# Two mixing blocks on one core: part of the first experts' weights loaded before the last attention values, router products and an embedding product reordered, the first expert's products put between the halves of its gather

## The reference, cut to what matters

```python
for i in range(DEPTH):                       # 2 layers
    h = rmsnorm_2(x, norm_mix[i]); proj = h @ w_in[i]
    y_a = neighbourhood_attention(...) @ w_na_o[i]
    y_b = latent_attention(...) @ w_mla_o[i]
    x = x + (sigmoid(gate_a) * y_a + sigmoid(gate_b) * y_b) @ w_out[i]
    x = x + expert_choice_moe(rmsnorm_2(x, norm_moe[i]), w_router[i], w1[i], w3[i], w2[i])
    x = x + sigmoid(rmsnorm_2(x, norm_ple[i]) @ ple_gate_w[i]) * (p[i] @ ple_w[i])

def expert_choice_moe(h, w_router, w1, w3, w2):      # 16 experts, 32 tokens each
    aff = softmax(h @ w_router)
    vals, idx = top_k(aff.T, 32); xg = h[idx]
    out = (silu(xg @ w1) * (xg @ w3)) @ w2           # each matrix 1024 x 1024, 4 MB
    return zeros.at[idx].add(out * vals)
```

## Time and profile before

| | us |
|---|---|
| median of 3 runs | 1897.53 |
| lowest and highest | 1896.41, 1899.77 |
| time of the profiled execution | 1900.6 |
| span of the profiled execution | 1898.8 |
| TensorE matmul busy | 1550.6 (82%) |
| VectorE busy | 612.3 (32%) |
| ScalarE busy | 500.4 (26%) |
| GpSimd busy | 193.9 (10%) |
| mean HBM traffic | 298 GB/s over the span |

### The profile page before, as it was taken

One profiled execution on the slowest core, in us unless ns is written; L12 is line 12 of the kernel. 1 busy time (PEld: TensorE's weight loads), 2 busy tenths in 40 slices (PEclk: granted clock), 3 DMA queues, 4 the chain that ended last, 5 costly groups with the idle time before them and its releaser, 6 DMA issues.

```text
span 1898.8 us, 29516 instructions
## 1 busy us (share of the span) xinstructions
PE 1550.6 (82%) x12506; PEld 1135.1 (60%) x12506; DVE 612.3 (32%) x923; ACT 500.4 (26%) x910; POOL 193.9 (10%) x214
## 2 busy tenths in 40 slices
PE   7999999999999999665655656999998666666656
PEld 6999899998898886232322323997883322323225
DVE  3456534577556353000000002655450000000005
ACT  3433333556444432000000002454330000000003
POOL 0043000011041100000000002410100000000003
PEclk9999999999999999898888888999999888989888
DMA  8564549432554569999999999545399999999994
GB/s 284 164 219 168 195 155 301 152 111 91 178 172 136 177 233 386 425 427 424 427 426 424 427 426 377 180 152 178 128 378 394 426 425 424 427 425 427 426 425 152
DMA packets 166894, 563.65 MB, mean 297 GB/s; under 512 B 10559, under 2 KB 120027, under 8 KB 133896
## 3 DMA queue, kind: packets, MB, share of 16 engines
q1 hardware_dynamic: 159012, 552.08, 75.1%
q10 hardware_dynamic: 7780, 10.10, 1.6%
HBM read 561.08 MB, written 5.23 MB: 298 GB/s over the span
## 4 chain that ended last, share of the span: by engine, by line
PE 52%; DMA 36%; DVE 4%; ACT 3%; issue 3%; POOL 1%; SPq 0%; ACTq 0%; DVEq 0%; POOLq 0%
DMA ring<-in_moe_w 36%; PE bank L965 21%; PE bank L1213 7%; PE bank L1622 5%; PE bank L921 4%; PE bank L1060 3%; PE bank L1645 2%; PE bank L1276 2%; ACT ring_r L1695 1%; ACT big L1743 1%; PE bank L1090 1%; PE bank L1480 1%; PE bank L1285 1%; PE bank L1037 1%; PE bank L1651 1%
## 5 line engine op out<-in xcount | busy, mean ns | idle before, releaser
L1622 PE MATMUL bank<-ring,big 128*32 128x256 f32 x3840 | 281.3, 443 | 195.7 <-DMA ring<-in_moe_w 193.2
L1622 PEld LDWEIGHTS bank<-ring,big 128*32 128x32 f32 x3840 | 147.0, 123 | 335.8 <-issue 295.4
L965 PE MATMUL bank<-big_r,ring_r 128*128 128x256 f32 (+1 forms) x2760 | 344.1, 285 | 0.0
L965 PEld LDWEIGHTS bank<-big_r,ring_r 128*128 128x128 f32 (+1 forms) x2760 | 335.1, 191 | 3.0 <-issue 2.2
L2092 DVE TENSOR_TENSOR ring_r<-ring,ring_r 128x2048 fp32r<-128x2048 f32 (+2 forms) x105 | 243.0, 2319 | 135.3 <-ACT ring_r L1695 133.9
L1743 ACT ACTIVATE big<-bank 128x512 f32<-128x512 f32 (+2 forms) x186 | 87.9, 491 | 571.6 <-PE bank L921 366.8
L1695 ACT ACTIVATE ring_r<-ring 128x2048 fp32r<-128x2048 f32 (+2 forms) x109 | 204.2, 1881 | 10.4 <-DMA ring<-in_ev_w_out 5.1
L1645 PE MATMUL bank<-ring,big 128*32 128x512 f32 x1024 | 136.7, 634 | 74.0 <-DMA ring<-in_moe_w 55.5
L2479 DVE SCALAR_TENSOR_TENSOR big<-big,bank 128x256 f32<-128x256 f32 x32 | 13.5, 421 | 463.9 <-ACT big L1995 463.9
L1213 PE MATMUL bank<-ring_r,big_r 128*128 128x512 f32 x576 | 135.7, 395 | 0.7 <-DVE big_r L2099 0.7
L921 PE MATMUL bank<-big 128*128 128x128 f32 (+6 forms) x636 | 105.1, 292 | 35.7 <-ACT big L1743 18.2
(11 more groups left out here) (204 smaller groups left out, 1512.8 us busy)
## 6 DMA issues: line engine op xcount, KB each, us to landing
ring<-in_moe_w SPq DMA_DIRECT2D x120, 2048.0 KB, 23.7
ring<-in_moe_w SPq DMA_DIRECT2D x128, 1024.0 KB, 24.9
ring<-in_w_in SPq DMA_DIRECT2D x28, 1024.0 KB, 5.4
ring<-in_od_w_in SPq DMA_DIRECT2D x22, 1024.0 KB, 6.5
ring<-in_ev_w_in SPq DMA_DIRECT2D x20, 1024.0 KB, 7.3
big<-in_moe_w SPq DMA_DIRECT2D x8, 2048.0 KB, 11.2
ring<-in_ev_w_out SPq DMA_DIRECT2D x8, 1024.0 KB, 5.0
ring<-in_od_cmp_w SPq DMA_DIRECT2D x8, 1024.0 KB, 8.1
```

The lines of the kernel that those rows point to most:

```text
L965: ins = unit[0].mark(mm(dst, lhsT, rhs, start=start and n == 0, stop=stop and n == len(terms) - 1))
L1622: ins = mm(banks[5 + up][32 * j:32 * j + 32, 0:256], xg[:, k, q, :], wv[:, r, 256 * j:256 * (j + 1)], start=k == 0, stop=k == KC - 1)
```

## The change

It has five parts, in each of the two layers.

1. SyncE: ahead of the load of `ple_w` (unit `("pw", 0)`) it waits for the last scores (`sc_done`) and then loads three quarters of spare 1 (`spare(1, r0=1)`, 1.5 MB) and all of spare 2 (2 MB). Where both were loaded, after the last values, only the remaining quarter of spare 1 is (`spare_row(1)`, 0.5 MB).
2. TensorE: the logits of tile 0 are made in pieces of 2 and 6 chunks instead of 4 and 4; the logits of tile 1 come ahead of `embed(0)`, which comes after `aff_T(0)`, and `embed(1)` comes after `aff_T(1)`.
3. TensorE: the gather is cut after 6 of its 8 chunks. In the first batch the order is gather 0 to 5, first half of `w1`, gather 6 and 7, first half of `w3`, second half of `w1`, second half of `w3`. In the later batches the order is gather 0 to 5, first half of `w1`, gather 6 and 7, and the rest as it was.
4. The second half of the gather goes to bank 7 instead of bank 6.
5. VectorE: the first batch is written out ahead of the loop, which runs over three batches.

```diff
+                    if unit == ("pw", 0):
+                        sp.wait_ge(sc_done, att_at(l, NAH + MLH))
+                        spare(1, r0=1)
+                        spare(2)
...
                 sp.wait_ge(pv_read, att_at(l, NAH + MLH))
-                spare(1)
-                spare(2)
+                spare_row(1)
                 deep(ups[0], first, 4)
                 sp.wait_ge(merged, 4 * (l + 1))
                 spare(0)
...
                 raw_T(l, 1, 0)
-                logits(l, 0, 0, 4)
+                logits(l, 0, 0, 2)
                 raw_T(l, 1, 1)
-                logits(l, 0, 4)
+                logits(l, 0, 2)
...
+                logits(l, 1)
                 unit[0] = Unit()
                 wait_bank(l, "pw", 0)
-                embed(0)
-                logits(l, 1)
...
                 aff_T(0)
+                embed(0)
+                aff_T(1).then_inc(rtT, 1)
                 embed(1).then_inc(proj_done, 1)
-                aff_T(1).then_inc(rtT, 1)
                 project(l, "pw", 1)
...
+                    def gather(k0, k1):
+                        for k in range(k0, k1):
+                            for t in range(TT):
+                                ins = mm(banks[4 + 3 * (k // 4)][:, (k % 4) * P:(k % 4 + 1) * P], u[:, t, k * P:(k + 1) * P],
+                                         onehot[:, t].rearrange("p q s -> p (q s)"), start=t == 0, stop=t == TT - 1)
+                            if k % 4 == 3:
+                                ins.then_inc(gathered, 1)
+
+                    gather(0, 6)
                     for q in range(BATCH):
                         m = l * NE + b * BATCH + q
...
+                        order = list(itertools.product(range(2), range(2)))
+                        if q == 0 and isinstance(b, int):
+                            order.sort(key=lambda e: e[1])
+                        for up, part in order:
+                            if q == 0 and part == up == 0:
+                                pe.wait_ge(xg_ready, 2 * g4 + 1)
+                            elif q == 0 and (up, part) == order[1]:
+                                gather(6, 8)
+                            if q == 0 and part == 1 and up == 0:
+                                pe.wait_ge(xg_ready, 2 * g4 + 2)
...
-                with dve.Fori(0, NE // BATCH) as b:
+                def batch(b):
...
+                batch(0)
+                with dve.Fori(0, NE // BATCH - 1) as b:
+                    steps.enter(b, BATCH)
+                    batch(b + 1)
+                    steps.leave(NE // BATCH - 1)
```

More of the change, by code:

```diff
@@ L787, in _, with spare, spare_row @@
             for l in range(LAYERS):
+                first = l * NE * D
+                ups = [a["moe_w1_2"], a["moe_w3_2"]]
+                def spare(i, r0=0):
+                    row = first + (i // 2) * D + 512
+                    src = flat(ups[i % 2])[row:row + 4 * P, :].rearrange("(p r) c -> p (r c)", r=4)
+                    sp.dma_start(view(spare_at[i], P, 4 * D)[:, D * r0:], src[:, D * r0:]).then_inc(spare_in[i], 16)
+                def spare_row(i):
+                    row = first + (i // 2) * D + 512
+                    src = flat(ups[i % 2])[row:row + 4 * P, :].rearrange("(p r) c -> p (r c)", r=4)
+                    sp.dma_start(view(spare_at[i], P, D), src[:, 0:D]).then_inc(spare_in[i], 16)
                 for unit in LAYER_UNITS:
+                    if unit == ("pw", 0):
+                        sp.wait_ge(sc_done, att_at(l, NAH + MLH))
+                        spare(1, r0=1)
+                        spare(2)
                     name, i = unit[0], unit[1]
@@ L803, in _ @@
                         tall_l(a["w_out_2"], l, D, 0, D, OUT_ROWS[2][unit[2]][0], 256, split=True)
[L804 to L810, removed]
                 def down(row):
@@ L909, in __init__ @@
                 def __init__(s, l, i):
-                    pe.wait_ge(spare_in[i], 16 * (l + 1))
+                    pe.wait_ge(spare_in[i], 16 * (2 if i == 1 else 1) * (l + 1))
                     s.words, s.first, s.step = view(spare_at[i], P, 4, D), True, Unit.before
@@ L1610, in batch @@
+                    gather(0, 6)
                     for q in range(BATCH):
                         m = l * NE + b * BATCH + q
[L1612 to L1625, removed]
+                        order = list(itertools.product(range(2), range(2)))
[8 more added lines that the diff above has]
+                                pe.wait_ge(xg_ready, 2 * g4 + 2)
+                            spare = isinstance(b, int) and q < 2 and part == 1
+                            U = Spare(l, 2 * q + up) if spare else Unit(double=True)
+                            wv = U.at(P, 4, D)
+                            for r in range(4):
+                                k = 4 * part + r
+                                for j in range(4):
+                                    ins = mm(banks[5 + up][32 * j:32 * j + 32, 0:256], xg[:, k, q, :],
+                                             wv[:, r, 256 * j:256 * (j + 1)], start=k == 0, stop=k == KC - 1)
+                                    U.mark(ins)
+                            if part == 1:
+                                ins.then_inc(up_done, 1)
@@ L2462, in _ @@
                 stand(dve)
-                with dve.Fori(0, NE // BATCH) as b:
+                def batch(b):
                     g4 = l * (NE // BATCH) + b
-                    steps.enter(b, BATCH)
                     V.tensor_tensor(onehot, con("iota").unsqueeze(1).unsqueeze(1).broadcast_to([P, TT, BATCH, CAP]),
-                                    idxT[:, :, bass.ds(b * BATCH, BATCH)].unsqueeze(3)
+                                    (idxT[:, :, b * BATCH:(b + 1) * BATCH] if isinstance(b, int) else
+                                     idxT[:, :, bass.ds(b * BATCH, BATCH)]).unsqueeze(3)
                                     .broadcast_to([P, TT, BATCH, CAP]), ALU.is_equal).then_inc(onehot_ready, 1)
@@ L2472, in _ @@
                         V.tensor_tensor(xg[:, 4 * n:4 * n + 4].rearrange("p k q s -> p k (q s)"),
-                                        banks[4 + 2 * n][:, :].rearrange("p (k s) -> p k s", k=4),
+                                        banks[4 + 3 * n][:, :].rearrange("p (k s) -> p k s", k=4),
                                         gm[:, 4 * n:4 * n + 4].unsqueeze(2).broadcast_to([P, 4, BATCH * CAP]),
@@ L2487, in _ @@
                             dve.wait_ge(comb_psum, m + 1)
-                    steps.leave(NE // BATCH)
+                batch(0)
[3 more added lines that the diff above has]
+                    steps.leave(NE // BATCH - 1)
                 for t in range(TT):
```

## The result

| | before | with the change |
|---|---|---|
| median of 8 runs each, side by side | 1897.76 us | 1902.11 us |
| lowest and highest | 1893.93, 1900.70 | 1899.89, 1905.30 |
| ratio | | 1.0021, interval 1.0012 to 1.0030 |
| time and span of the profiled execution | 1900.6, 1898.8 | 1900.54, 1898.7 |

The account below looks back on a forecast made before the run. TensorE was taken to bound the kernel before the experts, full DMA engines at 426 GB/s within them. Terms of 0.46 - 0.20 + 0.08 = +0.34 us a layer, +0.7 in all, gave 1898.2 us; range 1893.2 to 1901.2.

Parts of the forecast that it names:

- Regimes: TensorE is busy all the time before the experts' weight stream; from 760 to 1160 us the DMA engines are full, 426 GB/s.
- the point to follow: SyncE's issue at 740.25 us, after TensorE releases the first slots, restarts the weight stream and ends the hole from 739.4.
- Spares at 0: Loading spares 1 and 2 earlier gains 0, since the next load, at 696.16 us, waits for a ring slot.
- Rival A: Early spare bytes leave the experts' stream: up to 17.2 us gained over two layers, 1880.3 us; chance 0.05.
- Router order, +0.46: On TensorE before the top-k's transposes, embed(1) adds 0.73 us and earlier logits save 0.27: +0.46 us a layer.
- The clock: In the router's part, a fall to 1.2 GHz costs about 1 us and may come or go in either layer.
- Gather, +0.08: From the gather's start to the second unit of the first expert, 5.59 us instead of 5.51: +0.08 us a layer.
- VectorE's batch, -0.20: Writing VectorE's first batch out of the loop starts the one-hot product earlier: -0.20 us, between 0 and -0.30.
- The sum of the path: Router, VectorE and gather terms together: 0.46 - 0.20 + 0.08 = +0.34 us a layer, +0.7 for both.
- Rival C: The late embed(0) starves the weight stream: 2 x 2.4 = 4.8 us slower, 1902.3 us; chance 0.08.
- the late slots: embed(0) frees its slots later, opening a hole of about 1.1 us near 725 us, hidden with 1.3 us of slack.
- Range: Median time of the changed kernel from 1893.2 to 1901.2 us, with the clock counted as +-1 us a layer.

Follow-up runs that it names:

- embed(0) repeated early: The whole change with embed(0) made a second time, the extra one between the two tiles' logits; ratio to the kernel before 1.0017 (1.0008 to 1.0026).
- embed(0) repeated late: The whole change with embed(0) made twice in a row behind the first aff_T; ratio to the kernel before 1.0021 (1.0012 to 1.0031).
- embed(1) behind: The kernel before with only the second aff_T moved ahead of embed(1); ratio to the kernel before 1.0049 (1.0032 to 1.0066).
- version meant to be better: The kernel before plus VectorE's first batch written out, the cut gather, keep_x and keep_after pieces moved, slots freed earlier; ratio 1.0000 (0.9990 to 1.0011).
- run with 6.8 us at the lower clock: The whole change with embed(0) again between the two tiles' logits, embed(1) still behind the second aff_T; ratio to the kernel before 1.0034 (1.0022 to 1.0047).

## Why the prediction was wrong

- **Regimes and the point to follow: right.** The stream keeps 426 GB/s, the hole is still there, and the end moves by what the load after the hole moves: the markers add up to 3.8 us, the measured loss is 2.3 to 5.7.
- **Spares at 0: right,** alone and within the change. Rival A would have given a gain; the row at 693.61, with idle DMA engines for 7 us ahead of it, shows why not. The Trainium skill ("DMA: Bandwidth & Descriptors", "Rules for kernel authors") says to issue early and wait late, so that the setup cost overlaps; loads issued 8.4 us earlier (21.55 us ahead of the ring load instead of 13.20) brought nothing here, ratio 1.0001 (0.9993 to 1.0010).
- **Router order, +0.46: the path right, its size twice too large.** `embed(1)` behind the second `aff_T` costs +0.86 (I took 0.73), measured in a layer without a fall. The second `aff_T` starts 28.57 us behind the marker's start instead of 29.19, that is -0.62 (I took -0.27 for the logits). Together +0.24. No layer with the new order was free of a fall, so this sum was never measured as it stands; but the same sum gives 44.09 + 0.23 + 0.86 + 0.38 - 0.21 = 45.35 for the run with embed(0) repeated early, whose second `aff_T` starts at 29.42, and 45.36 was measured.
- **The clock: the step that failed.** The prediction saw the fall in one of two layers, priced it at about 1 us, and then wrote that it "may come or go in either layer", +-1 for the range and 0 in the sum. It was no such chance. It came in all 8 layers traced of the kernels whose TensorE order up to that point is the new one (the change twice, the router order alone, embed(0) repeated late). Where the order up to that point is the old one it came in 3 of 14: in 1 of the 10 layers of before, the early spares, the gather, VectorE's first batch and the change without its router part, and in 2 of the 4 layers of "embed(1) behind" and of the version meant to be better, which differ from before only behind the point where the fall begins. It costs 1.44 us for the twelve passes shown above; by the markers, what is left after the path's terms is 1.5 us a layer in the change, 1.4 and 1.2 in its repeat, 1.3 and 1.2 with the router order alone. The prediction's own 1 us in both layers would have made the forecast 1900.2. That the clock is a part of the loss in time is not shown by times, only by these rows: the kernel without a fall, 1.0017, and the change, 1.0021 and 1.0031, are not told apart.
- **Gather, +0.08: too small,** measured +0.38 and +0.37. The counting of passes was right; what was missing is a cost at each change between gather and unit. Gather to unit is 2.93 instead of 2.88, unit to gather 1.86 instead of 1.75, gather to unit 1.09 instead of 0.96.
- **VectorE's batch, -0.20: right,** -0.21.
- **The sum of the path: right by luck.** 0.24 + 0.38 - 0.21 = +0.41 a layer against the +0.34 predicted, but the router term was 0.22 too high and the gather term 0.30 too low.
- **Rival C, the late slots: right that they are hidden.** The new hole is there (721.3 to 724.0, 215 GB/s), and the 16 MB still end ahead of the restart (47 GB/s from 738.6 to 740.0). C's time, 1902.3, is almost the measured one, by another mechanism; that is chance.
- **Range:** +0.34 a layer was 1.9, of which about 1.5 is the clock. With 0.41 + 1.5 the sum would have given 1901.6 on the median of 1897.8, inside the measured interval; since 1.5 is what was left over in the same markers, this checks only that markers and time agree.

What starts the fall stays open. In all 14 falls it began 27.1 to 28.2 us behind the marker's start, from the end of the row of logits to the wait ahead of the second `aff_T`. It came with the 28 narrow passes in a row in 8 of 8 layers; in 1 of 2 with 24 in a row; in 2 of 4 with `embed(0)` between the tiles' logits and tile 0 in pieces of 2 and 6; in 3 of 14 with the old order. In the four layers of the change and its repeat, whose instructions up to there repeat within 0.02 us, it began anywhere from 27.65 to 28.24, so something beside the order of the program has a part. Its length does go with the wait: 6.8 us in the 3 falls where nothing stands in the wait ahead of the second `aff_T`, 3.4 us in the 11 others. The Trainium skill ("TensorE: Matmul & The Clock Gate", "What's actually happening") has activity release the clock from a low default. The trace agrees only so far that fewer falls came with a wide product among the narrow ones; TensorE's busy time would not have warned, since in the 4 us right ahead of the fall it was 3.76 to 4.00 us with the new order and 4.00 before, and in 22 to 26 us behind the marker's start it was 3.94 with the new order and also in the run without a fall.

## What to carry to other kernels

Ahead of a stream that is bound by bandwidth, loading earlier is worth something only if the load that waits for a place comes earlier too: look for what frees the first place, not for idle transfer time. Where TensorE's work is narrow and near a wait, wide products that look like filling may be worth keeping: with one moved out of the stretch the clock fell in every layer traced, and a fall cost more than the product takes. A fall seen once in the trace of before is a warning about exactly that stretch. And when the expected effect is a few tenths of a microsecond, measure it between two points of the trace a few tens of microseconds apart: total times moved by 7 us between runs of one kernel, the markers mostly by less than 0.2.

## What the runs showed of the hardware that was not expected

- TensorE's clock fell to 1.2 GHz for 3.4 us, or twice that, behind a row of products of 16 columns, although TensorE had been busy for 3.76 to 4.00 of the 4 us ahead of the fall. All 14 falls began 27.1 to 28.2 us behind the marker's start. With four wide passes placed 2.5 us earlier in the changed kernel there was none in two layers.
- In the run with 6.8 us at the lower clock, 12 passes of 128x256 took 5.30 us; with 3.4 us they took 4.20, without a fall 2.76.
- VectorE's entry into a loop cost 0.2 us more than the same instruction ahead of it.
- 3.67 million bytes moved into the attention's last heads, where 374 GB/s then flowed, changed TensorE's pace there by nothing that the trace shows (66.57 us from the first load of `w_out` to the first ring load in every trace).
